# Attention A, B and D in pairs of heads, with V stationary in P.V

## The reference

```python
# A (MLA): 8 heads, q/k of 64 + 32 (rope) = 96, v of 64; chunk-causal mask
# B: 8 heads of 64, learned relative bias, chunk-causal
# C: 4 heads, each two maps of 64 (softmax p0 - lambda * p1), v of 128, then RMSNorm of the head's output
# D: 8 query heads of 64 on 2 k/v heads, window of 128 keys and a left chunk, t5 bias, a sink a head in the softmax
sc = jnp.einsum('bqhd,bkhd->bhqk', q, k) + bias          # masked with -1e30
p = softmax(sc)                                           # D: over [sc, sink], sink dropped
o = jnp.einsum('bhqk,bkhd->bqhd', p, v)
merged = sum over branches of sigmoid(gate) * (o @ w_branch)
```

## Time and profile before

| | |
|---|---|
| runs | 3383.46, 3387.37, 3392.98 us |
| profiled execution | 3384.38 us, its span 3382.8 us |
| TensorE busy | 88% of the span (weight loads 68%) |
| VectorE, ScalarE, GpSimd busy | 60%, 46%, 17% |
| mean granted clock of TensorE | 0.939 of full |
| DMA | 199 GB/s in the mean, near 360 in the experts |
| stages of the first layer | A 167 to 290, gbA to 352, B to 490, gbB to 557, C to 645, D to 775, gbD and output projection to 870 us |
| stages of the second layer | A 1812 to 1937, B 2000 to 2138, C 2205 to 2294, D 2294 to 2424 us |

### The profile page before, as it was taken

How to read it: one execution, slowest core, us unless ns; L and a number is a source line. 1 busy time by engine, 2 the same in 40 slices (tenths; PEclk the granted TensorE clock), 3 DMA queues, 4 the chain that set the end, 5 groups by cost and what they waited for, 6 DMA issues and landing times. The chain is left out here.

```text
span 3382.8 us, 41792 instructions
## 1 busy us (share of the span) xinstructions
PE 2989.3 (88%) x13540; PEld 2291.4 (68%) x13540; DVE 2044.8 (60%) x2874; ACT 1543.7 (46%) x2382; POOL 578.2 (17%) x561
## 2 busy tenths in 40 slices
PE   2899998899879999999369999988998899999983
PEld 1587776577667777777256877756776677777762
DVE  4544345544458888888345444464445788888854
ACT  0342333332337777777023323243323577777740
POOL 0000000000043333333010000000002343333320
PEclk9899999999889999999669999998998899999985
DMA  8123223123359999998321232321334799999944
GB/s 205 55 88 123 101 100 115 67 85 133 122 191 362 367 368 368 361 361 320 153 69 69 88 137 84 128 80 62 111 106 186 264 364 360 359 370 363 366 162 174
DMA packets 119233, 671.92 MB, mean 199 GB/s; under 512 B 27372, under 2 KB 28652, under 8 KB 84364
## 3 DMA queue, kind: packets, MB, share of 16 engines
q1 hardware_dynamic: 86476, 608.19, 48.9%
q0 software_dynamic: 31456, 57.70, 5.1%
q10 hardware_dynamic: 1152, 4.19, 0.3%
HBM read 655.20 MB, written 56.98 MB: 211 GB/s over the span
## 5 line engine op out<-in xcount | busy, mean ns | idle before, releaser
L1725 DVE TENSOR_TENSOR ew_lo<-ew,e_hi 128x2048 fp32r<-128x2048 f32 x256 | 586.6, 2292 | 189.1 <-ACT e_hi L1584 188.9
L659 PE MATMUL bank<-h_hi,w_hi 128*128 128x512 f32 x1248 | 513.1, 411 | 35.5 <-DVE gt L742 12.1
L1584 ACT ACTIVATE e_hi<-ew 128x2048 fp32r<-128x2048 f32 x256 | 489.9, 1914 | 104.0 <-PE bank L1870 80.1
L659 PE MATMUL bank<-h_hi,w_lo 128*128 128x512 f32 x1248 | 510.0, 409 | 0.0
L659 PE MATMUL bank<-h_lo,w_hi 128*128 128x512 f32 x1248 | 505.4, 405 | 0.0
L593 DVE TENSOR_TENSOR w_lo<-raw,w_hi 128x1024 fp32r<-128x1024 f32 x198 | 242.6, 1225 | 430.6 <-ACT w_hi L585 430.4
L1870 PE MATMUL bank<-e_hi,x_hi 128*128 128x512 f32 x1024 | 413.3, 404 | 0.0
L1870 PE MATMUL bank<-ew_lo,x_hi 128*128 128x512 f32 x1024 | 402.4, 393 | 0.0
L1870 PE MATMUL bank<-e_hi,x_lo 128*128 128x512 f32 x1024 | 400.2, 391 | 0.0
L976 ACT ACTIVATE pr<-sn,negmax 128x256 f32<-128x256 f32 (+3 forms) x256 | 138.4, 541 | 421.2 <-DVE negmax L967 421.2
L1493 POOL DMA_INDIRECT y_d<-y,idx x128 | 217.6, 1700 | 621.5 <-issue 524.0
(11 more groups left out here) (286 smaller groups left out, 4648.6 us busy)
## 6 DMA issues: line engine op xcount, KB each, us to landing
ew<-in_wexp SPq DMA_DIRECT2D x128, 2048.0 KB, 10.1
raw<-in_wmix SPq DMA_DIRECT2D x294, 512.0 KB, 4.0
ew<-in_wexp SPq DMA_DIRECT2D x128, 1024.0 KB, 10.1
yt<-y_d SPq DMA_DIRECT2D x8, 3072.0 KB, 10.1
ada<-in_ada SPq DMA_DIRECT2D x4, 2048.0 KB, 18.2
ew<-in_wexp SPq DMA_DIRECT2D x2, 3072.0 KB, 10.4
h_d<-htok ACTq DMA_DIRECT2D x8, 512.0 KB, 2.6
v_d<-vB SPq DMA_DIRECT2D x1, 3840.0 KB
```

Source lines behind the costliest of these rows:

```text
L659: ins = nc.tensor.matmul(out, lhs, rhs, start=start, stop=stop)
L1584: nc.scalar.activation(e_hi[h][:], up_part(ew, j, h), ACT.Copy).then_inc(whi_done, 1)
L1725: nc.vector.tensor_tensor(up_part(ew_lo, j, h), up_part(ew, j, h), e_hi[h][:].bitcast(F32), ALU.subtract).then_inc(wlo_done, 1)
```

## The change

A, B and D now have 16 groups of two maps as C has: heads 2p and 2p + 1 with the same queries. In a step TensorE does both scores of g + 1, twice as many products as before, both transposes of g (into the two banks `TB`, lane 0 and 1), and values of both maps of g - 1. ScalarE copies lane 0 to `pt[0]`, VectorE lane 1 to `pt[1]`, in every step.

In values, V (128 keys x 64) is stationary and the transposed probabilities (128 keys x 128 queries) move. The result has the head's 64 values on partitions, 0 to 63 for the first head and 64 to 127 for the second, and the queries along the free axis: already turned. So the four transposes of a set go. In their place the reciprocals of the row sums, which lie on partitions by query, are spread by `pe_spread_sums`: eight matmuls with a column of `rcp` broadcast to 64 columns as stationary and the identity moving, into `MB`. `dve_sums` makes the reciprocals as soon as the group's exponentials are done (with D's sinks, `act_sinks`). `act_take_set` copies `OB` to `on` on ScalarE, `dve_scale_set` multiplies it by `MB`, and the split reads `on` instead of `MB`. The next set's first values wait for `act_take_set`. C is computed as before.

The bias tables have four slots instead of two; the two new ones lie where k of A (for `tab`) and q of C (for `tabD`) have been, and are filled with -1e30 by GpSimd once all scores of A, or of C, are issued. The column of `sinkt` and the order of maps follow the new numbering.

```diff
-    return [Map(br, h, qb) for h in range(8) for qb in range(TC)]
+    return [Map(br, 2 * p + par, qb) for p in range(4) for qb in range(TC) for par in range(2)]
...
-GROUP0 = {"A": 0, "B": 32, "C": 64, "D": 80}
-NGROUP = {"A": 32, "B": 32, "C": 16, "D": 32}
-PER_SET = {"A": 8, "B": 8, "C": 4, "D": 8}
+GROUP0 = {"A": 0, "B": 16, "C": 32, "D": 48}
+NGROUP = 16
+PER_SET = 4
...
 def group_maps(g):
-    if g < 64:
-        return [g]
-    return [64 + 2 * (g - 64), 65 + 2 * (g - 64)] if g < 80 else [96 + g - 80]
+    return [2 * g, 2 * g + 1]
+
+
+def lanes_of(g):
+
+    return (g % 2,) if branch_of(g) == "C" else (0, 1)
...
+        tab = tab + [place(f"tab{2 + i}", [P, S], at=r0 + 24576 + 2048 * i) for i in range(2)]
+        tabD = tabD + [place(f"tabD{2 + i}", [P, 2 * P], at=r0 + 1024 * i) for i in range(2)]
...
+            elif kind == "ot" and n // 4 == 2:
+                eng.wait_ge(olo_ready, n + 1)
             elif kind == "ot":
-                eng.wait_ge(olo_ready, n + 1)
+                eng.wait_ge(on_ready, n + 1)
...
-                    dve.wait_ge(tab_in[th % 2], 32 * (th // 2 + 1))
+                    dve.wait_ge(tab_in[th % 4], 32 * (th // 4 + 1))
                 elif br == "D":
-                    dve.wait_ge(tabD_in[mp.head % 2], 32 * (mp.head // 2 + 1))
-            bias = {"A": tabA[:, S - mp.nk:], "B": tab[mp.head % 2][:, S - mp.nk:], "C": tab[mp.head % 2][:, S - mp.nk:],
-                    "D": tabD[mp.head % 2][:, 2 * P - mp.nk:]}[br]
-            floor = sinkt[:, u - MAP0[br]:u - MAP0[br] + 1] if br == "D" else BIG
+                    dve.wait_ge(tabD_in[mp.head % 4], 32 * (mp.head // 4 + 1))
+            bias = {"A": tabA[:, S - mp.nk:], "B": tab[mp.head % 4][:, S - mp.nk:], "C": tab[mp.head % 4][:, S - mp.nk:],
+                    "D": tabD[mp.head % 4][:, 2 * P - mp.nk:]}[br]
+            col = TC * mp.head + mp.qb
+            floor = sinkt[:, col:col + 1] if br == "D" else BIG
...
-                act.wait_ge(tr_ready, map_group(u - 4) + 1)
+                act.wait_ge(tr_ready, TURNED[(u - 4) // 2 + 1])
...
         def pe_transpose_probs(pe, br, g):
-            u = group_maps(g)[0]
-            mp = MAPS[br][u - MAP0[br]]
-            if br == "C":
-                pe.wait_ge(comb_ready, g - GROUP0["C"] + 1)
-            else:
-                pe.wait_ge(p_ready, u + 1)
-            if g >= 2:
-                pe.wait_ge(pt_copied[g % 2], g // 2)
-            for b in range(mp.nk // P):
-                ins = nc.tensor.transpose(TB[g % 2][:, b * P:(b + 1) * P], pr[u % 4][:, b * P:(b + 1) * P], ident)
-            ins.then_inc(tr_ready, 1)
...
+            for m in lanes_of(g):
+                u = group_maps(g)[0 if br == "C" else m]
+                mp = MAPS[br][u - MAP0[br]]
+                if br == "C":
+                    pe.wait_ge(comb_ready, g - GROUP0["C"] + 1)
+                else:
+                    pe.wait_ge(p_ready, u + 1)
+                if LANE_N[m][g]:
+                    pe.wait_ge(pt_copied[m], LANE_N[m][g])
+                for b in range(mp.nk // P):
+                    ins = nc.tensor.transpose(TB[m][:, b * P:(b + 1) * P], pr[u % 4][:, b * P:(b + 1) * P], ident)
+                ins.then_inc(tr_ready, 1)
...
+        def copy_probs(eng, g, m):
+
+            br = branch_of(g)
+            nk = MAPS[br][group_maps(g)[0] - MAP0[br]].nk
+            eng.wait_ge(tr_ready, TURNED[g] + lanes_of(g).index(m) + 1)
+            if LANE_N[m][g]:
+                eng.wait_ge(pv_done, max(h for h in range(g) if m in lanes_of(h)) + 1)
...
         def pe_values(pe, br, g):
 
-            u = group_maps(g)[0]
-            mp = MAPS[br][u - MAP0[br]]
+            mp = MAPS[br][group_maps(g)[0] - MAP0[br]]
             i = g - GROUP0[br]
-            o = SET0[br] + i // PER_SET[br]
-            if i % PER_SET[br] == 0 and o:
-                pe.wait_ge(on_ready, o)
-            pe.wait_ge(pt_copied[g % 2], g // 2 + 1)
-            w = 2 * DH if br == "C" else DH
-            col = i % PER_SET[br] * w
-            head = mp.head // 4 if br == "D" else mp.head
+            o = SET0[br] + i // PER_SET
+            if i % PER_SET == 0 and o:
+                if branch_of(g - 1) == "C":
+                    pe.wait_ge(on_ready, o)
+                else:
+                    pe.wait_ge(o_out, o if o <= 8 else o - 4)
+            for m in lanes_of(g):
+                pe.wait_ge(pt_copied[m], LANE_N[m][g + 1])
+            q = slice(mp.qb * P, (mp.qb + 1) * P)
             nb = mp.nk // P
             for b in range(nb):
-                ins = nc.tensor.matmul(OB[:, col:col + w], pt[g % 2][:, b * P:(b + 1) * P],
-                                       V_[br][:, mp.k0 // P + b, head * w:(head + 1) * w], start=b == 0, stop=b == nb - 1)
+                kb = mp.k0 // P + b
+                if br == "C":
+                    ins = nc.tensor.matmul(OB[:, q], pt[g % 2][:, b * P:(b + 1) * P],
+                                           vC[:, kb, mp.head * P:(mp.head + 1) * P], start=b == 0, stop=b == nb - 1)
+                else:
+                    for m in range(2):
+                        head = mp.head // 4 if br == "D" else mp.head + m
+                        ins = nc.tensor.matmul(OB[DH * m:DH * m + DH, q], V_[br][:, kb, head * DH:(head + 1) * DH],
+                                               pt[m][:, b * P:(b + 1) * P], start=b == 0, stop=b == nb - 1)
             ins.then_inc(pv_done, 1)
...
+        def pair_sets(o):
+
+            return o + 1 if o < 8 else o - 3
 
         def set_maps(o):
-            br = "ABCD"[o // 4]
-            n = len(MAPS[br]) // 4
...
+        def dve_sums(dve, o):
+
...
+            dve.wait_ge(p_ready, u0 + n)
+            if o >= 12:
+                pair = o - 12
+                sink = vec[:, V_SINK + 8 * pair:V_SINK + 8 * pair + 8].rearrange("p (h q) -> p q h", h=2)
+                nc.vector.tensor_tensor(sinkt[:, 32:40].rearrange("p (q h) -> p q h", h=2),
+                                        negmax[:, u0:u0 + n].rearrange("p (q h) -> p q h", h=2), sink,
+                                        ALU.add).then_inc(es_in, 1)
                 dve.wait_ge(es_ready, o - 11)
                 link(dve, nc.vector.tensor_tensor(psum_of[:, u0:u0 + n], psum_of[:, u0:u0 + n], sinkt[:, 40:48], ALU.add))
...
-                dve.wait_ge(pv_done, GROUP0[br] + (o % 4 + 1) * PER_SET[br])
-                if o:
-                    dve.wait_ge(on_ready, o)
-                link(dve, nc.vector.reciprocal(rcp[:, 0:8], psum_of[:, u0:u0 + n]))
             if o:
                 wait_mb_full(dve, ("ot", o - 1))
-            if br == "C":
-                nc.vector.tensor_tensor(on[:], OB[:].rearrange("p (q c) -> p q c", q=TC),
-                                        rstd[:, 4:8].unsqueeze(2).broadcast_to([P, TC, P]), ALU.mult).then_inc(on_ready, 1)
-            else:
-                nc.vector.tensor_tensor(on[:].rearrange("p q (h c) -> p h q c", h=2),
-                                        OB[:].rearrange("p (h q c) -> p h q c", h=2, q=TC),
-                                        rcp[:, 0:8].rearrange("p (h q) -> p h q", h=2).unsqueeze(3).broadcast_to(
-                                            [P, 2, TC, DH]), ALU.mult).then_inc(on_ready, 1)
...
+            nc.vector.reciprocal(rcp[:, 0:8], psum_of[:, u0:u0 + n]).then_inc(sums_ready, 1)
+
+        def act_sinks(act, o):
+            if o >= 12:
                 act.wait_ge(es_in, o - 11)
                 nc.scalar.activation(sinkt[:, 40:48], sinkt[:, 32:40], ACT.Exp).then_inc(es_ready, 1)
+
+        def pe_spread_sums(pe, o):
+
+            pe.wait_ge(sums_ready, pair_sets(o))
+            wait_mb_free(pe, ("ot", o))
+            for q in range(TC):
+                for m in range(2):
+                    ins = nc.tensor.matmul(MB[DH * m:DH * m + DH, q * P:(q + 1) * P],
+                                           rcp[:, 2 * q + m:2 * q + m + 1].broadcast_to([P, DH]), ident,
+                                           start=True, stop=True)
+            ins.then_inc(m_full, 1)
+
+        def act_take_set(act, o):
+
+            act.wait_ge(pv_done, PER_SET * (o + 1))
+            if o == 12:
+                wait_mb_full(act, ("ot", o - 1))
+            elif o:
+                act.wait_ge(olo_ready, o)
+            nc.scalar.activation(on[:].rearrange("p q c -> p (q c)"), OB[:], ACT.Copy).then_inc(o_out, 1)
+
+        def dve_scale_set(dve, o):
+            dve.wait_ge(o_out, pair_sets(o))
+            wait_mb_full(dve, ("ot", o))
+            v = on[:].rearrange("p q c -> p (q c)")
+            nc.vector.tensor_tensor(v, v, MB[:], ALU.mult).then_inc(on_ready, 1)
+
+        def dve_norm_set(dve, o):
+            dve.wait_ge(ss_ready, o - 7)
+            nc.vector.tensor_scalar(stat[:, 4:8], rcp[:, 12:16], 1.0 / P, EPS, ALU.mult, ALU.add).then_inc(ms2_ready, 1)
+            dve.wait_ge(rs2_ready, o - 7)
+            nc.vector.tensor_tensor(on[:], OB[:].rearrange("p (q c) -> p q c", q=TC),
```

(78 more changed lines are left out.)

70 lines of the change are left out of this document (22 added, 48 removed).

## The result

The changed kernel takes 3296.85 us (median of 4 runs, 3294.84 to 3301.01) against 3387.51 for the kernel before (4 runs, 3383.46 to 3392.98). The ratio is 0.9733, with a 95% interval of 0.9716 to 0.9750: 90.7 us less, where 59.6 was forecast. The time lies in the range (3290 to 3392), but near its fast end and outside the band given to the forecast itself (3305 to 3350); it is 9 us from rival 4 and 31 from the forecast. The profiled execution took 3301.01 us, its span is 3299.4.

The account below looks back on a forecast made before the run. TensorE, 88% busy, was taken as the bound. Per layer, A 3.5, B 20.4, D 15.2, sets -9.4, starts -3.9 and waits 4 gave 29.8 us, 59.6 in all: 3328 us as a median, range 3290 to 3392.

Parts of the forecast that it names:

- rival 4: TensorE's old waits go nearly all, 24 us a layer instead of 4: 3288 us; chance 0.1.
- the two mechanisms of overlap: On TensorE, row halves (scores of B and D) and column halves (values of A, B, D) run side by side.
- Waits that go: TensorE's waits in B and D for `on`, reciprocals and P^T copies: 4 us a layer regained, bounds 0 and 24.
- sets: Set ends in A, B, D: transposes go, spread and two crossings come, 0.78 us more each, 9.4 a layer lost.
- starts: Stage starts of A, B, D: second group's scores wait for VectorE's bias of the first, 3.9 us a layer lost.
- this cover: 17 products, 3.9 us, on TensorE ahead of the next tile or values, half as many before; cost priced at 0.
- Scores in pairs: In B and D, two heads' scores run side by side on row halves: 14.2 and 11.6 us a layer gained.
- V stationary: Values in fully overlapping column halves, half of the records saved: 8.8, 8.8, 6.2 us a layer in A, B, D.
- crossings: Leaving or re-entering the full array, 0.165 us each: 5.3, 2.6, 2.6 us a layer lost in A, B, D.
- Rival 1: Column halves run one after the other, or loads stand between: 34.3 us a layer lost, 3396 us; chance 0.12.
- Rival 2: Next set's values wait for act_take_set on ScalarE: 56.6 us a layer lost, 3441 us; chance 0.08.
- Rival 3: The overlap holds but coarse steps eat half of it, 15 us a layer: 3358 us; chance 0.2.

Follow-up runs that it names:

- e7: Changed kernel with the old form of values and set ends, and one product between a pair's two scores in B and D: 3347.84 us, 0.9891.
- e6: Kernel before with the transposes of a set and the split of their result one step later in A, B and D: 3379.03 us, 0.9988.
- e8: Kernel before with copies of P^T ahead of the weight splits on ScalarE and VectorE in A, B and D: 3369.14 us, 0.9954.
- e9: Kernel before with no ada (modulation weight) tiles among the jobs that fill D's stage: 3406.18 us, 1.0062.
- e10: Changed kernel with pe_spread_sums moved next to values and no ada tiles among the jobs that fill D's stage: 3334.04 us, 0.9852.
- e3: Changed kernel with one product between the two scores of a pair in B and D: 3344.04 us, 0.9874.
- e2: Changed kernel with the old form of values (probabilities stationary, V moving) and set ends as before: 3309.64 us, 0.9760.
- e4: Changed kernel with every matmul of pe_spread_sums issued twice: 3327.48 us, 0.9817.
- e1: Changed kernel with all blocks of the first head's values ahead of the second's, instead of alternating: 3315.5 us, 0.9774.

## Why the prediction came out as it did

The direction, the two mechanisms of overlap and, to within 0.1 us, the price of every part of a step that the timelines show were right. The term that was mis-sized is "Waits that go": it took 4 us a layer from bounds of 0 and 24, and about 19 came. That the time still fell into the range is owed to the width of the range, not to this term: with half a chance on 3305 to 3350 the forecast leaned on the old waits staying. In the words of the list of rivals, rival 4 is what happened, on top of a forecast that else holds.

**Where the excess sits.** Without its 4 us the forecast is, by stage and with sets and starts, A +0.9 (-3.5 + 3.1 + 1.3), B -16.0 and D -10.8 (-15.2 + 4.4): 25.9 a layer. Measured were -1.2, -21.1 and -22.6. The excess is 2.1, 5.1 and 11.8, together 19.0. TensorE's waits for `pt` and `on` in these stages of the kernel before were 4.1 us in B (3.1 + 1.0) and 12.2 in D (5.1 + 4.8 + 2.3), and in A:

```profile
PE bank L1032 <- ACT pt L1014: 1.2, 1, 1.2
PE bank L1094 <- DVE on L1070: 1.0, 1, 1.0
```

2.2 us, which the prediction's bound left out (it counted B and D). The second layer reads 2.7, 3.8 and 12.1 for A, B and D. So the excess is, stage by stage, the size of the old waits. e7, which saves no matmul, shows it without subtracting forecasts: -18.3 a layer over the stages, and it has the new waits at the stages' starts to pay as well (3.2 in the changed kernel, below). Taken by e7, "Waits that go" is worth 18.3 + 3.2 = 21.5 a layer, still nearer to the upper bound than the subtraction says.

**Why they went.** The chain in the kernel before is plain in its timeline of D (last field: idle before, and the releaser):

```profile
699.75 1.28 DVE L790 CUSTOM_DVE_ANT_0 raw<-raw,cb,vec 128x1024 f32<-128x1024 f32 x1
...
701.22 0.91 SPq L572 DMA_DIRECT2D raw<-in_wmix  x2
...
704.91 1.06 ACT L585 ACTIVATE w_hi<-raw 128x1024 fp32r<-128x1024 f32 x1 [3.31 <-DMA raw<-in_wmix]
706.00 1.23 DVE L593 TENSOR_TENSOR w_lo<-raw,w_hi 128x1024 fp32r<-128x1024 f32 x1 [4.95 <-ACT w_hi L585]
707.14 0.42 DVE L1016 COPY pt<-bank 128x256 f32<-128x256 f32 x1
707.61 0.66 PE L1032 MATMUL bank<-vD,pt 128*128 128x64 f32 x4 [2.72 <-DVE pt L1016]
```

A weight tile comes late. Its transfer is only issued at 701.22, right behind the operation at line 790 with which VectorE gives back the buffer of an ada tile, and it is there 3.7 us later. SyncE's queue waits for such operations most of the stage:

```profile
SPq L572 <- DVE mod L790: 128.1, 8, 27.5
```

So the chain begins in VectorE's own queue, at the place that the ada work has in it. Then ScalarE stands at the tile's split, VectorE at the second half of it; the copy of P^T is queued behind; TensorE's values wait 2.72 us for a tile that isn't theirs. A fourth `raw` buffer, or the ada work further ahead in VectorE's queue, would go at the root; no run tried either. In the changed kernel the tiles of D are no earlier. Rows of the view of waits, ScalarE in stretch D, before:

```profile
ACT w_hi L585 <- DMA raw<-in_wmix: 11.8, 4, 4.2
```

and after:

```profile
ACT w_hi L596 <- DMA raw<-in_wmix: 17.6, 5, 4.8
```

ScalarE waits longer than before, 17.6 us instead of 11.8, and TensorE no longer feels it: it has 17 products, 3.9 us, between a step's copies and their user, about the 4.8 of the longest wait (in e7 the longest is 5.0, and the cover about the same). I had listed this cover as protection of the new kernel ("if it is gone, the price is that of rivals 2 and 3") and priced it as safety; it was a gain, since the old cover of 8 or 9 products, 2 us, was already too short for waits of 4.2. e6 and e8 moved one user or one producer in the old queues and the wait came back elsewhere (none and 16 us gained); e7 lengthened the distance for all at once. e9 and e10 take D's late tiles away instead: 9.4 us a layer for the old kernel in that stage, next to nothing for the new one, which had that already. That the longer distance in time is what does it is the reading that fits these runs; e7 changes the distance together with all else that two heads a step bring.

**Scores in pairs.** Forecast B 14.2 and D 11.6, 51.6 in all. Taking the pairing away costs 40 to 48 us from the changed kernel (e3: B 13.3, D 9.0) and 44 between e2 and e7 (B 14.2, D 6.1). B is right. D is smaller than its sum, I can't say by which record; a step of D has less work, so an engine that owes something may end it.

**V stationary, crossings, sets.** Forecast 8.8 + 8.8 + 6.2 - 5.3 - 2.6 - 2.6 - 9.4 = 3.9 a layer. e2 measures at most 9 us in the whole and 5.9 a layer in the stages, which agrees with 3.9 but not beyond noise. Overlap is full (0.87 us for sixteen records), a crossing costs 0.14 and 0.17 where I had 0.165, a set's spread 1.12 where I had 1.2. All the effort of this half of the change buys a tenth of the result or less; of the 23.8 us a layer that the overlap was forecast to give, 10.5 go to the crossings of the steps and 9.4 to the ends of sets.

**Starts.** Forecast 3.9 a layer; the first layer shows 1.3 in D and 1.3 and 0.6 in A and B, by the views of waits of their stages: 3.2.

**The rivals.** Rival 1 (column halves serial) fell at 1.03 us. The Trainium skill's page TensorE: Matmul & The Clock Gate, Part 3, The mechanism, has a weight load overlap a matmul in flight only if the row group differs. By this rule there would be no pairs in 0.107 us here; the trace doesn't agree, records of two column halves come at one in 54 ns (0.87 / 16, e4). Its 2.38 for three column tiles, scaled to an estimate of 1.59 for two, is too low for these two: 16 x 0.107 / 0.87 is 2.0. Rival 2 (the hand-over of a set) shows in no wait of TensorE for ScalarE's copy of OB. Rival 3 (coarse steps eat half) has the sign wrong: coarse steps gave 34 to 37 us (e7). Rival 4 gave 3288, 9 us from the result, and had a chance of 0.1; its rows were there to be read.

**What stays open.** Whether V stationary is worth anything in the total, which part of the coarser step does the work, why D's pairing is worth less than its columns, and how much of the 19 us a layer is the clock rather than the waits themselves: the wait records sum to 18.5, of which 1.4 is left, so the clock would have about 2. In D alone the granted clock would allow more, (1 - 0.94) x 130 = 7.8 us of lost clock in the stretch before against (1 - 0.97) x 114 = 3.4 after. No run separated the two.

## What to carry to other kernels

When a change makes steps coarser, count the work that stands between every producer and its user in the in-order queues, before and after, and hold it against the longest wait in the trace, not the mean: if the old distance was shorter than that wait and the new one is about as long, book most of the wait as gain. Then follow the late transfer back to what held its buffer: it may be an instruction in one of the same queues. Moving one instruction in such a queue mostly moved the wait here (e6, e8); the distance has to grow for all. And two matmuls that each use half of the array, by rows or by columns, cost one here when they stood next to each other in the queue, so collect everything that uses halves in one place, and alternate the halves matmul by matmul (e1). Last, measure a changed kernel twice before reading differences of 10 us in 3300 between versions.

## What the runs showed of the hardware that was not expected

- Two column halves overlap fully with 128 moving columns: 16 more records cost 0.87 us (e4), one in 54 ns, where one alone is 0.107, with each load of 64 columns hidden.
- The order within the queue matters by its length. Head by head, eight records (four and four) cost 0.60 us against 0.58 when alternating, but twelve 1.07 against 0.81 and sixteen (eight and eight) 1.52 against 1.03; in e1 only four records of values start in the first half microsecond:

```profile
229.72 0.65 PE L1052 MATMUL bank<-pt,vA 128*64 128x128 f32 x4
```

- Going into column halves costs 0.09 to 0.14 us and coming back 0.16 to 0.17, together about as much as for row halves, where the two came to 0.33 (0.10 in, 0.23 out); putting two such stretches together saved 0.30 us in the step shown.
